# Loading every second streamed weight chunk by two transfers of 120 and 8 rows

## The reference, cut to what matters

```
q = h @ w_query                       # 8 heads x 2 halves x 128
top-16 of 128 keys per half -> 256 sums -> top-16 experts, softmax gates
u_sel, v_sel = u[expert], v[expert]   # 128 experts per token, 1024 floats each, twice
act = gelu(h . u_sel);  y = sum (gate * act) * v_sel
```

## Time and profile before

| | |
|---|---|
| median of three runs | 1829.98 us |
| span of the profiled execution | 1826.5 us |
| median less span (start and end around the span) | 3.5 us |
| PE busy | 1366.8 us, 75% |
| DVE busy | 1169.7 us, 64% |
| ACT busy | 597.3 us, 33% |
| POOL busy | 551.0 us, 30% |
| moved by DMA | 681.29 MB, 373 GB/s on average |
| queue 0 (gathers) | 553.68 MB, 73.6% of 16 engines |
| queue 1 (SyncE) | 126.23 MB, 18.0% of 16 engines |

### The profile page before, as it was taken

How to read it: one execution, slowest core, us unless ns; L and a number is a source line. 1 busy time by engine, 2 the same in 40 slices (tenths; PEclk the granted TensorE clock), 3 DMA queues, 4 the chain that set the end, 5 groups by cost and what they waited for, 6 DMA issues and landing times.

```text
span 1826.5 us, 21618 instructions
## 1 busy us (share of the span) xinstructions
PE 1366.8 (75%) x7080; PEld 550.5 (30%) x7080; DVE 1169.7 (64%) x2705; ACT 597.3 (33%) x1530; POOL 551.0 (30%) x633
## 2 busy tenths in 40 slices
PE   8999999988874545698678865776787765655566
PEld 7856666653430010122122221221232210101011
DVE  5831334277776777656786647767877577677764
ACT  2421011124342323433443323433443333333332
POOL 2001232023332333322433224322342333333331
PEclk9999999999996676799777878897898977666677
DMA  9048697559999999999999999999999999999997
GB/s 358 5 176 345 204 373 263 230 211 419 420 420 419 417 415 417 420 417 409 417 392 418 416 418 406 419 417 416 384 410 418 420 421 421 421 422 418 418 421 292
DMA packets 118194, 681.29 MB, mean 373 GB/s; under 512 B 11790, under 2 KB 13970, under 8 KB 50114
## 3 DMA queue, kind: packets, MB, share of 16 engines
q0 software_dynamic: 78336, 553.68, 73.6%
q1 hardware_dynamic: 39745, 126.23, 18.0%
HBM read 678.30 MB, written 1.05 MB: 372 GB/s over the span
## 4 chain that ended last, share of the span: by engine, by line
DMA 37%; PE 29%; DVE 13%; ACT 4%; issue 3%; DVEq 3%; POOL 2%; ACTq 1%; POOLq 0%
DMA big<-in_peer_uv,expert 33%; PE ps L662 7%; DVE big L675 6%; PE ps L1900 6%; PE ps L1889 6%; PE ps L824 5%; DMA normed<-in_peer_uv,expert 5%; DVEq L528 2%; POOL big L634 2%; PE ps L647 2%; DVE residual L722 1%; ACT placed L706 1%; ACT L706 1%; ACT placed L710 1%; ACT L683 1%
## 5 line engine op out<-in xcount | busy, mean ns | idle before, releaser
L662 PE MATMUL ps<-big,placed 128*32 128x512 f32 x1992 | 596.1, 795 | 393.9 <-ACT placed L710 391.8
L675 DVE CUSTOM_DVE_ANT_0 big<-big,ps 128x1024 f32<-128x1024 f32 x498 | 595.7, 1219 | 340.4 <-DMA big<-in_peer_uv,expert 322.9
L634 POOL DMA_INDIRECT big<-in_peer_uv,expert x498 | 473.8, 951 | 1016.7 <-PE ps L662 855.9
L706 ACT ACTIVATE placed<-sel,dots 128x32 f32<-128x32 f32 x512 | 163.5, 319 | 797.2 <-DVE dots L675 789.6
L662 PEld LDWEIGHTS ps<-big,placed 128*32 128x32 f32 x1992 | 80.8, 122 | 820.5 <-ACT placed L710 734.7
L824 PE MATMUL ps<-big 128*128 128x512 f32 x384 | 187.2, 624 | 2.5 <-DVE big L1129 1.4
L710 ACT ACTIVATE placed<-placed,gate 128x32 f32<-128x32 f32 x512 | 164.6, 321 | 35.4 <-issue 0.3
L1900 PE MATMUL ps<-big,sc 128*128 128x512 f32 x256 | 115.5, 595 | 0.0
L1889 PE MATMUL ps<-ua,big 128*128 128x256 f32 (+1 forms) x512 | 110.4, 370 | 2.9 <-PEq L75 2.9
L824 PEld LDWEIGHTS ps<-big 128*128 128x128 f32 x384 | 69.8, 196 | 116.6 <-issue 108.7
L1889 PEld LDWEIGHTS ps<-ua,big 128*128 128x128 f32 x512 | 94.1, 194 | 27.8 <-issue 17.7
(11 more groups left out here) (371 smaller groups left out, 1280.2 us busy)
## 6 DMA issues: line engine op xcount, KB each, us to landing
big<-in_mlp_w SPq DMA_DIRECT2D x16, 2048.0 KB, 15.9
big<-in_peer_wq SPq DMA_DIRECT2D x2, 8192.0 KB, 26.9
big<-in_w_kv SPq DMA_DIRECT2D x32, 512.0 KB, 14.2
big<-in_peer_wq SPq DMA_DIRECT2D x32, 512.0 KB, 13.2
big<-in_w_in SPq DMA_DIRECT2D x5, 2048.0 KB, 17.8
big<-in_peer_uv,expert POOLq DMA_INDIRECT x530, 15.0
big<-in_w_q SPq DMA_DIRECT2D x16, 512.0 KB, 14.0
big<-in_w_o SPq DMA_DIRECT2D x16, 512.0 KB, 10.3
```

The lines of the kernel that those rows point to most:

```text
L634: nc.gpsimd.indirect_dma_start(out=pair_row(n), out_offset=None, in_=rows, in_offset=bass.IndirectOffsetOnAxis(ap=expert[:, n // TOPK % DE ...
L662: last = nc.tensor.matmul(acc[r:r + TOK, :], placed[:, n % RING, :], pair_row(n)[:, D + BANK * half:D + BANK * (half + 1)], start=(opens a ...
L675: nc.vector.tensor_tensor_reduce(out=row, in0=row, in1=rows_x, scale=1.0, scalar=0.0, op0=ALU.mult, op1=ALU.add, accum_out=dots[:, u % 2, ...
L706: a.activation(to, sel32[:], ACT.Gelu, scale=dots[:, u % 2, k:k + 1])
```

## The change

Chunks with an odd number (48 of 96) are loaded by two transfers, rows 0 to 119 and rows 120 to 127, into the same buffer and counted on the same semaphore. Chunks with an even number are loaded as before. The wait of a product counts 16 for each transfer into its buffer. As six is even, the odd buffers of the ring hold odd chunks only. Nothing else is changed.

```
+        def weight_parts(c):
+            return ((0, 120), (120, P)) if c % 2 else ((0, P),)
+        def weight_loads(c):
+            return 16 * sum(len(weight_parts(i)) for i in range(c % RING_W, c + 1, RING_W))
...
-            pe.wait_ge(S(f"w{c % RING_W}_loaded"), 16 * (c // RING_W + 1))
+            pe.wait_ge(S(f"w{c % RING_W}_loaded"), weight_loads(c))
...
-                    sp.dma_start(ring_w[c % RING_W], src).then_inc(S(f"w{c % RING_W}_loaded"), 16)
+                    for lo, hi in weight_parts(c):
+                        sp.dma_start(ring_w[c % RING_W][lo:hi], src[lo:hi]).then_inc(S(f"w{c % RING_W}_loaded"), 16)
```

## The result

The changed kernel took 1950.24 us (median of four runs, 1942.51 to 1954.6) against 1830.62 us for the kernel before on the same chip. The ratio is 1.0653, with a 95% interval of 1.0627 to 1.0678. That is 119.6 us more, or 2.49 us for each of the 48 odd chunks. I had forecast 1852 us and a range up to 1910 us. The direction was right and the size was off by a factor of five (119.6 us for 22.1). The time lies above even the 1935 us of the rival with the full price, though within its open band (anything from 1885 us).

What follows compares the result with a forecast made beforehand. It took full DMA engines, moving rows back to back, as the bound. 7.8 + 10.4 + 3.9 = 22.1 us on the 1826.5 us span, with the median 3.5 us above the span, gave 1852 us; range 1832 to 1910 us.

Steps and rivals of the forecast that it cites:

- the rival with the full price: Split chunks' rows: sharing partitions costs the 103 us upper bound plus 7.8; 1935 us, anything from 1885; chance 0.20.
- What bounds the kernel: From 412 to 1800 us: all 16 DMA engines move rows back to back, at 384 to 422 GB/s.
- Issue and signals: SyncE's 48 more DMA issues and the added small packets: costed at nothing, 41 us at most if cover were gone.
- That sign: TensorE waiting tens of us for chunks would mean the second transfer's issue or landing is the cause.
- How many engines: Odd chunks: 120 rows on 15 engines, eight on eight; the same eight get ninth rows, 7.8 us more.
- What one row costs: Split chunks' rows meeting at shared partitions: 10.4 us for the 120-row parts, 3.9 us for the 8-row parts.
- my upper bound: Split chunks' rows: 48 x (8 + 1) rows, each up to 239 ns longer, 103 us.
- the 0.34: Share of time a sharer is on a weight row, 163 of every 480 ns, used to scale the sharing cost.
- Row count alone: Odd chunks: rows still cost 163 ns and only the ninth row counts; 1838 us, chance 0.23.
- No change: Extra rows vanish in the 1.4% between 416 and 422 GB/s; 1830 us, chance 0.10.
- faster: One DMA engine gets none of the odd chunks, which helps if it is the slow one; 1824 us, chance 0.06.
- The signs that I named: Stretches with weights: about 400 GB/s, share near 1.00 if rows stick, queue 1 rows about 190 ns; later stretches 420 to 422.

Runs made afterwards that it cites:

- the pair of kernels with eight extra rows: Kernel before plus an unused 8-row transfer per odd chunk, to partitions 32, 36, ... 60 (1836.88 us) or 120 to 127 (1853.46 us).
- the loads alone: Separate kernel without the computation, 24 transfers of a kind at once: 128 rows 1.27 us, 120 rows 2.08 us; into DRAM both equally fast.
- 120 rows only: Changed kernel without the 8-row transfer, so rows 120 to 127 of odd chunks are not loaded: 1909.31 us against 1828.15.
- 64 + 64: Odd chunks in two transfers, rows 0 to 63 and 64 to 127, against the kernel before: 1933.94 us, ratio 1.0577.

## Why the prediction was wrong

**What bounds the kernel** was read rightly. The DMA engines are full, row by row, and slower rows show in the time: 115 us more of packets' time, 120 us more in all.

**Issue and signals** were rightly put near nothing: splitting by columns adds 48 issues and more signals, for 6 us, which holds the shorter packets too. I had said that TensorE would wait only a few us for chunks; it was 70.8 us. And I had said that tens of us would mean that the issue or the landing of the second transfer was the cause. That sign was badly chosen: 81 of the 120 us stay with one transfer a chunk, and with split columns TensorE waited 92.3 us at a cost of 6 us.

**How many engines** was right, by the 336 packets. The term that came of it, 7.8 us, agrees with the 8.9 us measured (5.1 to 10.2 by the interval). That it is the same engines each time is not shown by this, since a second transfer costs up to 6 us by the split columns, and ninth rows that went round all engines would have cost 4 us.

**What one row costs** is the term that failed. I had 10.4 + 3.9 = 14.3 us; what is left of the 119.6 us after the ninth rows is about 111 us. Two things were wrong in the step. First, I counted only the rows of the split chunks as slowed. The gathers' rows were put at nothing. By the place reading, an engine that writes to another's place takes time from that engine's gather rows, and an engine that is stuck on a weight row has its own gather row behind it. I had written the latter in a rival, "for it", and named a small rise of queue 0's rows as a sign, but put neither into any sum. Measured over odd and even chunks together, the gathers' rows went from 317 to 420 ns and the chunks' rows from 163 to 207 ns. One turn of the two queues takes 627 ns for 480, and 8 turns for each of 96 chunks give 8 x 96 x 147 ns = 113 us. Of these, 8 x 96 x 103 ns = 79 us are gathers' rows, for which the sum had nothing, and 8 x 96 x 44 ns = 34 us are chunks' rows, for which it had 14.3 us. Second, for the same reason my upper bound, 103 us, was none: it covered nine rows on one queue. A bound on a shared resource has to hold all that is in flight there, here 8 KB rows that are twice as long. Nor was 402 ns the price of a fully crowded row: with 16-row transfers one behind another and nothing else, each engine took 0.55 us for its one row.

I also thinned the sharing by the 0.34 of the time in which a weight row is in flight, as if the gathers between made it weaker. It went the other way: in the three kernels whose odd chunks are split by rows into two transfers, the loss in the loop was 1.8 times the loss of the same transfers alone. A likely reason is that what a place loses while engines meet elsewhere finds no idle time later in which to be made up; no run takes this apart.

**The rivals.** Row count alone fits as a term and is wrong as the whole. Crowded rows at the full price was the right mechanism and still too cheap. No change and faster were wrong; the DMA share of 1.02 left nothing to win from an engine with less to do.

**The signs that I named.** GB/s fell to 315 to 320 where I had said about 400, at a share of 1.02, which was to mean stuck rows. Queue 1's row took 207 ns where I had said 190. (My own 10.4 us are 27 ns on each row of an odd chunk, 190 ns for it but 177 ns over odd and even chunks, which is what the view shows.) Stretches without chunks nearly kept their rate, 417 to 418 GB/s for 420.

**What stays open.** The trace names no engine and no place. That the partitions decide is shown by the pair of kernels with eight extra rows, which differ in nothing else, and for the split itself by the loads alone, where 120 rows are slow into the chip and not into DRAM. Which partitions make up a place is inferred from rates: 412, 209, 119 and 56 GB/s for 128, 32 or 64, 16 and 8 rows. Why the loss in the loop is 1.8 times that alone with two row parts, 2.1 times for 120 rows only and 0.9 times for eight extra rows was not taken apart. Nor was it why eight rows cost some 40 us behind a transfer of 120 and 25 us behind one of 128; that the slow time reaches into the even chunks with 120 + 8 rows, and not with 64 + 64, may belong to it.

## What to carry to other kernels

Where DMA engines are full, load whole 128-partition tiles, or split by columns: a split by rows puts engines in each other's way, and it slows the other transfers in flight with it, at 1.8 times here what the split costs alone. When a page shows DMA at 9 tenths, read the GB/s line below it and divide share by rows: a full engine can be a slow one. And when bounding a cost on a shared resource, count the neighbours' work too.

## What the runs showed that was not expected

120 rows by 15 engines take 2.08 us where 128 rows take 1.27 us: fewer bytes, 64% more time. Even 112 rows (1.71 us) and 96 rows (393 KB at 252 GB/s, 1.56 us), which use all 16 engines, are slower than 128.

Something like it is seen at the end of the kernel before, on the reading side. The last store takes 32 rows from 32 partitions with nothing beside it. The DMA view of 1820 to 1826.5 us:

```profile
DMA packets 48, 0.13 MB, mean 20 GB/s; under 512 B 16, under 2 KB 16, under 8 KB 48
q1 hardware_dynamic: 48, 0.13, 9.2%
```

9.2% of 16 x 6.5 us over 32 rows is 299 ns a row. That is close to the 32-row loads alone, where 209 GB/s are 313 ns a row; one store is thin evidence that reading has the same limit.
